# Both pasts: the sums of exponents as a running row of 256 columns on GpSimd, in place of VectorE's sums over eight units

## The reference

```python
s = jnp.einsum('bqhd,bkhd->bhqk', q_i, k).astype(f32) * ATTN_SCALE
s = s + jnp.transpose(cq_i, (0, 2, 1))[..., None] - cum_k_t[:, :, None, :]
pr = jax.nn.softmax(s, axis=-1)
return jnp.einsum('bhqk,bkhd->bqhd', pr.astype(v.dtype), v)
```

## Time and profile before

| | us |
|---|---|
| median of 3 runs | 2555.01 (2551.08 to 2573.7) |
| the profiled execution | 2564.63 |
| its span, first to last instruction | 2562.8 |
| TensorE busy | 2239.9 |
| VectorE busy | 1418.7 |
| ScalarE busy | 884.1 |
| GpSimd busy | 373.4 |
| mean granted clock of TensorE | 0.921 |

### The profile page before, as it was taken

The page is one execution under the profiler, slowest core; times in us unless marked ns, Lnnn a source line. Parts: engine busy times, 40 slices in busy tenths (PEclk is TensorE's granted clock), DMA queues, the critical chain, the costliest instruction groups (busy, mean ns, idle before and its releaser), DMA issues. The chain is left out here.

```text
span 2562.8 us, 63697 instructions
## 1 busy us (share of the span) xinstructions
PE 2239.9 (87%) x26369; PEld 1728.9 (67%) x26369; DVE 1418.7 (55%) x2305; ACT 884.1 (34%) x1644; POOL 373.4 (15%) x426
## 2 busy tenths in 40 slices
PE   6798989989768996799999979999878866999997
PEld 3565877777538863577777757664766654777776
DVE  2436777777574546654422364557766666553333
ACT  2326544444322222243322231147444333332222
POOL 2003133333200000111100000014223310110000
PEclk8898999999868977899999989999988977999999
DMA  7413899999741024223323324460999961332321
GB/s 244 116 51 99 281 328 343 329 332 335 260 168 19 4 91 143 66 66 90 90 76 91 91 66 139 129 193 13 306 283 300 296 212 48 86 90 83 91 86 59
DMA packets 316331, 396.88 MB, mean 155 GB/s; under 512 B 25153, under 2 KB 234379, under 8 KB 316069
## 3 DMA queue, kind: packets, MB, share of 16 engines
q1 hardware_dynamic: 286356, 286.86, 36.4%
q0 software_dynamic: 29712, 106.25, 12.1%
HBM read 382.34 MB, written 10.70 MB: 153 GB/s over the span
## 5 line engine op out<-in xcount | busy, mean ns | idle before, releaser
L851 PE MATMUL bank<-yT,WH 128*128 128x288 f16 x3200 | 533.3, 290 | 47.4 <-DVE yT L705 34.6
L851 PEld LDWEIGHTS bank<-yT,WH 128*128 128x128 f16 x3200 | 314.5, 99 | 146.3 <-issue 51.7
L915 DVE SCALAR_TENSOR_TENSOR WL<-wring,WH 128x1024 f16<-128x1024 f32 x172 | 224.4, 1308 | 258.1 <-ACT WH L895 258.0
L1411 DVE TENSOR_TENSOR KL<-bank,KH 128x512 f16<-128x512 f32 x416 | 277.9, 685 | 152.0 <-ACT KH L1389 101.0
L1389 ACT CAST KH<-bank 128x512 f16<-128x512 f32 x416 | 237.3, 586 | 351.8 <-PE bank L1304 333.9
L851 PE MATMUL bank<-uT,WH 128*128 128x288 f16 x2048 | 338.4, 288 | 10.7 <-DVE WL L915 10.7
L851 PE MATMUL bank<-yT,WL 128*128 128x288 f16 x1600 | 331.5, 289 | 0.0
L895 ACT ACTIVATE WH<-wring 128x1024 f16<-128x1024 f32 x172 | 180.6, 1054 | 237.8 <-PE bank L851 221.4
L851 PEld LDWEIGHTS bank<-uT,WH 128*128 128x128 f16 x2048 | 201.7, 99 | 63.6 <-DVE WL L915 11.3
L851 PE MATMUL bank<-uT,WL 128*128 128x288 f16 x1024 | 211.2, 288 | 0.0
L851 PEld LDWEIGHTS bank<-yT,WL 128*128 128x128 f16 x1600 | 158.4, 99 | 42.0
(11 more groups left out here) (496 smaller groups left out, 4189.8 us busy)
## 6 DMA issues: line engine op xcount, KB each, us to landing
wring<-in_ada_w SPq DMA_DIRECT2D x96, 512.0 KB
vTd<-in_state_dil_k SPq DMA_DIRECT2D x160, 256.0 KB
yT<-in_cache_fox_k SPq DMA_DIRECT2D x128, 256.0 KB
krows<-in_cache_fox_k SPq DMA_DIRECT2D x128, 256.0 KB
wring<-in_mlp_up SPq DMA_DIRECT2D x64, 512.0 KB
wring<-in_mlp_down SPq DMA_DIRECT2D x64, 512.0 KB
wring<-in_ev_w_in SPq DMA_DIRECT2D x26, 512.0 KB
wring<-in_od_w_in SPq DMA_DIRECT2D x24, 512.0 KB
```

Of the source, the lines that this page charges most:

```text
L851: last = nc.tensor.matmul(bank[b + h][:, 0:HALF], w[s % 2][:, c, :], x[:, s % parts * KC + c, h * HALF:(h + 1) * HALF], start=(s % parts = ...
L915: nc.vector.scalar_tensor_tensor(WL[s % 2][:, :, :], w[:, :, :], WSCALE, WH[s % 2][:, :, :], ALU.mult, ALU.subtract).then_inc(w_free, 1)
L1411: nc.vector.tensor_tensor(KL[i][:, :], turned[n % NT][:, :], KH[i][:, :], ALU.subtract).then_inc(lo_out, 1)
```

## The change

The four (or three) part sums of a sequence on VectorE are gone. GpSimd keeps a row `run` of 256 columns for each sequence in their place: it adds group 1 to group 0, and then each further group of four units, seven adds in the even past and four in the odd one, each waiting for the one before it and for the exponents that it reads. In the odd past a row holds two units of 128 columns. These adds stand in GpSimd's queue ahead of V tile `sums_at` = 9 of each sequence in both pasts (`sums_at` is counted on over the sequences). VectorE's `whole_sum` then reduces the row to `csum` in the slot of the last part sum of before, and adds the new keys' exponents in an instruction of its own.

```diff
--- before.py
+++ after.py
@@ -1227,15 +1227,15 @@
             ST = [sb(sc, f"ST{i}", [P, nu + E, 64]) for i in range(2)]
             pmx = sb(sc, "pmx", [P, 2, NP, W])
             cmx, amx = maxima_home or [sb(sc, n, [P, 2, W]) for n in ("cmx", "amx")]
-            psm = sb(sc, "psm", [P, 2, NP, W])
+            run = sb(sc, "run", [P, 2, SG // E, W])
             csum = sb(sc, "csum", [P, 2, W])
             ainv = sb(sc, "ainv", [P, 2, E])
             OD = sb(sc, "OD", [P, NSEQ * E, P])
             v_in = list(v_first) + [sem(f"v_in{i}") for i in range(len(v_first), VR)]
             kt_ok, hi_out, lo_out, sc_ok, sc_out, new_out, v_used, o_ok, o_out = (
                 sem(n) for n in ("kt_ok", "hi_out", "lo_out", "sc_ok", "sc_out", "new_out", "v_used", "o_ok", "o_out"))
-            pmx_ok, cmx_ok, amx_ok, sub_ok, exp_ok, psm_ok, csum_ok, inv_ok, clear, back_ok, back_out = (
-                sem(n) for n in ("pmx_ok", "cmx_ok", "amx_ok", "sub_ok", "exp_ok", "psm_ok", "csum_ok", "inv_ok", "clear", "back_ok", "back_out"))
+            pmx_ok, cmx_ok, amx_ok, sub_ok, exp_ok, run_ok, old_sum, csum_ok, inv_ok, clear, back_ok, back_out = (
+                sem(n) for n in ("pmx_ok", "cmx_ok", "amx_ok", "sub_ok", "exp_ok", "run_ok", "old_sum", "csum_ok", "inv_ok", "clear", "back_ok", "back_out"))
             slots = N + VLAG
             LAST = NT_ - nt
             assert NT_ % KR == 0 and nt >= VR
@@ -1283,7 +1283,21 @@
 
                 @block.gpsimd
                 def _(pool):
+                    def running_sum(s):
+                        if s >= 2:
+                            pool.wait_ge(old_sum, s - 1)
+                        group = lambda g: ST[s % 2][:, g * SG:(g + 1) * SG, :].rearrange("p (t e) c -> p t (e c)", e=E)
+                        mine = run[:, s % 2, :, :]
+                        for g in range(1, NG):
+                            pool.wait_ge(exp_ok, s * NP + g // 2 + 1)
+                            if g > 1:
+                                pool.wait_ge(run_ok, s * (NG - 1) + g - 1)
+                            nc.gpsimd.tensor_tensor(mine, group(0) if g == 1 else mine, group(g), ALU.add).then_inc(run_ok, 1)
+
+                    sums_at = VR - 1 + -(-(nu + LAG + NP + 3 - VLAG) // TU)
                     for t in range(NT_):
+                        if t >= sums_at and (t - sums_at) % nt == 0:
+                            running_sum((t - sums_at) // nt)
                         if t % nt == VR - 1:
                             s = t // nt
                             pool.wait_ge(cmx_ok, 2 * s + 2)
@@ -1444,17 +1458,15 @@
                         nc.vector.tensor_tensor(v, v, amx[:, s % 2, :].unsqueeze(1).to_broadcast([P, (end_of(p) - lo_of(p)) // E, W]),
                                                 ALU.subtract).then_inc(sub_ok, 1)
 
-                    def part_sum(s, p):
-                        dve.wait_ge(exp_ok, s * NP + p + 1)
-                        if s >= 2 and p == 0:
-                            dve.wait_ge(csum_ok, s - 1)
-                        nc.vector.tensor_reduce(psm[:, s % 2, p, :].rearrange("p (e c) -> p e c", e=E),
-                                                ST[s % 2][:, lo_of(p):end_of(p), :].rearrange("p (t e) c -> p e c t", e=E), AX.X, ALU.add).then_inc(psm_ok, 1)
-                        if p == NP - 1:
-                            dve.wait_ge(psm_ok, (s + 1) * NP)
-                            if s >= 2:
-                                dve.wait_ge(o_ok, s - 1)
-                            nc.vector.tensor_reduce(csum[:, s % 2, :], psm[:, s % 2, :, :].rearrange("p t c -> p c t"), AX.X, ALU.add).then_inc(csum_ok, 1)
+                    def whole_sum(s):
+                        dve.wait_ge(run_ok, (s + 1) * (NG - 1))
+                        dve.wait_ge(exp_ok, (s + 1) * NP)
+                        if s >= 2:
+                            dve.wait_ge(o_ok, s - 1)
+                        nc.vector.tensor_reduce(csum[:, s % 2, :], run[:, s % 2, :, :].rearrange("p t c -> p c t"), AX.X, ALU.add).then_inc(old_sum, 1)
+                        dve.wait_ge(old_sum, s + 1)
+                        nc.vector.tensor_tensor(csum[:, s % 2, :], csum[:, s % 2, :], ST[s % 2][:, nu:nu + E, :].rearrange("p e c -> p (e c)"),
+                                                ALU.add).then_inc(csum_ok, 1)
 
                     def normalise(s):
                         o = mixed[:, :].rearrange("p (e c) -> p e c", c=256)
@@ -1477,8 +1489,8 @@
                         if 0 <= s < NSEQ:
                             if r < NP:
                                 less(s, r)
-                            if r % SUM_EVERY == SUM_EVERY - 1 and r // SUM_EVERY < NP:
-                                part_sum(s, r // SUM_EVERY)
+                            if r == SUM_EVERY * NP - 1:
+                                whole_sum(s)
                         n = i - VLAG - 1
                         if n >= 0 and n % nu == nu - 1:
                             normalise(n // nu)
```

## The result

| | before | after |
|---|---|---|
| median, us | 2553.05 (2547.99 to 2573.7) | 2728.73 (2720.03 to 2734.77) |
| ratio | | 1.0687 [1.0653, 1.0721] |
| span of the profiled execution, us | 2562.8 | 2727.3 |
| mean granted clock of TensorE | 0.921 | 0.893 |
| VectorE busy, us | 1418.7 | 1374.2 |

The account below looks back on a forecast made before the run. The prediction took TensorE's waits for VectorE's KL as the nearer limit in the even past, transfers in the odd. Even past 56, odd past 38, second MLP -2 gave 92 us over the 2555.0 median: 2647 us, range 2595 to 2705.

Parts of the forecast that it names:

- (a): Rival: only GpSimd's way back to adds is loaded, so no VectorE stall; 2565 us, chance 0.10.
- (b): Rival: nothing is loaded, the adds lie in GpSimd's idle time and VectorE is relieved; 2547 us, chance 0.04.
- (c): Rival: port or queue makes GpSimd's adds long, 1.5 us each; 2682 us, chance 0.06.
- The load: GpSimd idles 6.85 us at each change between all-reduce and adds, in both directions, priced from one MLP row.
- To the all-reduce: Even past, sequences 1 to 6: late all-reduce stalls TensorE 6.1 us, lower clock adds 2; 48.6 us.
- The clock: Half clock after each TensorE stall loses 2 us in the even past; none added in the odd past.
- V issue 9: Even past: load and adds hold this issue, its tile lands 0 to 2 us late; taken as 0.
- End of the even past: All-reduce 6.8 us late, then load and adds ahead of three V issues, taken as 5; together 12 us.
- Odd past: TensorE stalls 36.6, less 18 of key waits, plus 12 for held transfers and 10 at the end, less 3 relief: 38 us.
- Relief: Part sums off VectorE shorten TensorE's KL waits, 5 us in the even past and 3 in the odd.
- Second MLP: GpSimd arrives already set for adds, so of ScalarE's 6.79 us wait 2 us come back.
- Bounds: Worst cases behind the range of 2595 to 2705 us, which leaves out (a), (b) and the tails, 0.2.

Follow-up runs that it names:

- b_switch: The kernel before, part sums kept on VectorE, with one GpSimd addition of one column where the change puts its adds; 2679.26 us, ratio 1.0479.
- a_ksmall: The kernel after with the K transfers of both pasts cut to 16 of 1024 columns; 2708.77 us in a single run.
- a_hold: a_std with the first add of each sequence made eleven times more, so GpSimd holds V issue 9 with work; 2620.18 us, ratio 1.0281.
- a_sumlate: The kernel after with VectorE's whole_sum moved to the third slot from the sequence's end; 2723.33 us, ratio 1.0665.
- a_std: The kernel after with the all-reduce replaced by a GpSimd multiplication by 1.0, so no change of work inside a past; 2554.02 us, ratio 0.9993.
- b_std: The kernel before with the all-reduce replaced by the same GpSimd multiplication, as control for a_std; 2553.61 us, ratio 0.9998.
- v_run: The kernel before with a running row of 512 columns on VectorE in place of the part sums, nothing on GpSimd; 2552.60 us, ratio 1.0000.
- b_preload: The kernel before with a one-column GpSimd addition behind the last V issue of each past; 2548.42 us, ratio 0.9993.

## Why the prediction was wrong in size

The direction, the mechanism and the place were right: the pairs of MODIFY_POOL_CONFIG stand where it said, the standstill follows in both directions, and the rivals (a), one direction only, (b), none, and (c), adds of 1.5 us, are all false (the adds took 0.72, 0.85 with the wait for each other, as forecast). The size was 92 us for 176. b_switch splits the error by stage. The two standstills by themselves were forecast at 55 us in the even past and at 36.6 - 18 + 6.8 = 25 in the odd one, and cost 79.7 and 45.3: 44 us of error. What the adds and the held issue put on top was forecast at 0 and 12 and cost 21.5 and 25.5: 35 us. By its own steps:

**The load, 6.85 us both ways.** It took 9.04 us ahead of the adds and 7.54 ahead of the all-reduces. The one row it was priced by the earlier trace rows lies in an MLP; in a past, with its transfers, it is longer, and a_ksmall puts about 1 us of that down to traffic. This mis-sized every term it stood in. The stall of TensorE behind the all-reduce, forecast at 6.1 us in each of twelve sequences, was 6.2 to 8.3 us in five even ones (7.99 above) and 11.8, in a wait for `p`, in the other, and 7.5 to 9.2 in the six odd ones: 48.5 and 50.9 us for 36.6 each.

**To the all-reduce, 48.6 us in the even past.** b_switch has this term without the others: with the end's 6.8 the forecast was 55 us, and its even past is 79.7 longer. KL and `p` waits grew by 39.4 us there for 36.6, the end's wait by 6.4 for 6.8; what was too small is the term of the clock, 21.8 us more of busy time for 12, and some 12 us lie in small waits that weren't priced. In the kernel after, KL and `p` grew by 32.2: the six stalls are 48.5 us, and of the 31.6 us of waits before about half went.

**The clock, 2 us a stall in the even past, none in the odd one.** TensorE's busy time for the same instructions grew by 14.3 us in the even past, where 12 were forecast, and by 15.4 in the odd one, where the prediction said "The half clock after those waits is there already, so none is added". That step failed: the stage's mean granted clock fell from 0.91 to 0.81. Whatever the ten key waits of before had cost in busy time, the stalls behind the all-reduce and the row cost more.

**V issue 9, "just in time", 0 us.** This is the step whose reasoning failed. After, it is 60.5 us of waits for V, 55 more than before, in a stage that got 101 longer; without it and without the adds (b_switch) the stage is 21.5 us shorter. Two estimates in it were each a little short: the hold was 14.8 us for 12.8 (14.5 and 12.5 later than before), and the room that was left was taken at its edge. After, the tile was due 14.7 us after the time at which issue 9 would have followed issue 8 (377.68 to 392.37, where TensorE's wait begins), and a tile took 5.9 to land, here and in the earlier trace rows; that leaves 8.8, and the hold takes 14.5: 5.7 late, the measured wait. With the row of before (17.5 us from issue to use) the same sum gives 2.9. The 0 to 2 us of the prediction came from a hold that was 2 us too short and from the reading that a thing just in time costs nothing. The one shown is among the shortest: the seven waits ahead of the end are 5.7 to 9.0 us, 47.6 together. a_hold shows the term by itself, 34.5 us in this past.

**End of the even past, 12 us.** This term was about right. TensorE waited 10.4 us for the first exponents (3.7 before) and 12.1 for the last V, where the kernel before has 6.3 us of waits for V, all of them here: 6.7 and 5.8 make 12.5 more.

**Odd past, 38 us; it was 71.** The 18 us regained from the key waits were right (21.5). The term for held transfers was 12 us and stood for V not being asked for; V made no wait of note here. What the hold did was another thing, and the prediction had it only for the end: the row was not done when VectorE reached `whole_sum`, which kept the slot of the last part sum. VectorE waited 44.3 us in eight waits, with KL queued behind it. A second stall of TensorE follows in each of seven sequences, 2.6 to 3.5 us in six and 6.9 in the last of them, 25.8 together. In the trace of after, POOL and then DVE in an odd sequence:

```profile
1979.42 0.72 POOL L1295 TENSOR_TENSOR run<-ST 128x256 f32<-128x256 f32 x1 [8.21 <-issue]
1980.28 2.46 POOL L1295 TENSOR_TENSOR run<-run,ST 128x256 f32<-128x256 f32 x3
...
1982.77 0.42 DVE L1466 TENSOR_REDUCE csum<-run 128x128 f32<-128x256 f32 x1 [4.21 <-POOL run L1295]
```

The prediction should have named what is queued behind `whole_sum` and when the last add ends in every sequence, not in the last alone. But in a_sumlate, where the second stalls are gone, at most some 5 us came back, and why is open. By b_switch the larger part of the odd past's error is in the all-reduce's own term, with the busy time that comes with it: 45 us for 25.

**Relief, 8 us.** None could be measured: a_std and b_std are 0.4 us apart with some 9 us of uncertainty on each, and v_run is before to within 5.6. TensorE's KL waits did fall, 12.3 to 8.2 us in the even past and 15.8 to 11.9 in the odd one (b_std to a_std), which is the size that the prediction gave them; that it reached the end isn't shown. **Second MLP, 2 us:** b_preload has it at none that can be told.

**Bounds.** The range took 2 us a sequence for V waits as its worst case. Seven of them are 14 us, where 47.6 were measured; with these in its place 2705 would have been 2739. Its 6 to 10 us for an even sequence were too low as well, before any wait for V: b_switch has (79.7 - 6.4) / 6 = 12.2.

## What to carry to other kernels

An engine's idle time is free only if what it is asked to do is of the kind that it does already: look for the instruction that stands at each change of kind (here the MODIFY_POOL_CONFIG pair) and count the changes that the edit makes in the loop, whatever the size of the work between them; here sixteen additions of one column cost 4.8%. It's the changes that count and not the instruction: in the second MLP of the kernel before 64 of them stand before additions, and only the first was followed by a standstill. Where an engine also issues transfers, sum all that is put ahead of one issue and hold the sum against the time to the tile's use less its landing time; when that comes out as "just in time", price the overrun at the pessimistic end of each part, as two holds that fit one by one may not fit together. And before work is taken off an engine, ask what its waits would be replaced by: 43 us off VectorE were worth nothing that could be measured here.

## What the runs showed of the hardware

GpSimd's change between `partition_all_reduce` and additions costs 6 to 11 us in these pasts, on every change and not only on the first: in the kernel after 8.0 to 10.9 us towards additions, 9.0 in the mean, and 6.2 to 9.4 towards the all-reduce, 7.5 in the mean; 8.0 and 6.9 in the one run with less traffic (154 GB/s for 261 in the even past). The Trainium skill, GPSIMD Engine Reference, section 2.1 (Instruction dispatch), gives about 6 us for the first call to a freshly loaded kernel, with no visible instruction; the kind agrees, but here it comes at every change, the sizes are up to 1.8 times as large, and the direction matters. Issues of indirect DMAs between two all-reduces, or between two additions, brought no pair with them: in a_std, additions and such issues alternate through both pasts, with 0.01 us from the issue to the first addition in the sequence shown and 0.4 us in all sixteen.

The standstill is invisible in the busy times, and the page of the profile leaves the line out as one of its smaller groups. In the view of a line it is an "issue" ahead of the work: 144.6 us for 11.5 us of additions.
